# Reading the down weights of a routed expert layer in 16 KB runs, with every eighth gate and up column as stationary

## The reference, cut to what matters

```python
hid = silu(einsum('becd,edf->becf', xs, w_gate)) * einsum('becd,edf->becf', xs, w_up)
ye = einsum('becf,efd->becd', hid, w_down) * gsel[..., None]
# added back at the tokens' rows, then the gated residual; the same for both layers
```

## Time and profile before

| | |
|---|---|
| median of three runs | 1824.03 us (1822.21 to 1824.89) |
| the profiled execution's own time | 1824.63 us |
| its span, first to last instruction | 1822.8 us |
| mean granted TensorE clock | 0.972 |
| TensorE matmul busy | 1624.9 us, 89% |
| TensorE weight load busy | 1289.1 us, 71% |
| VectorE, ScalarE, GpSimd busy | 829.4, 572.0, 388.4 us |
| moved by DMA | 502.58 MB, 276 GB/s over the span |

### The profile page before, as it was taken

The page is one execution under the profiler, slowest core; times in us unless marked ns, Lnnn a source line. Parts: engine busy times, 40 slices in busy tenths (PEclk is TensorE's granted clock), DMA queues, the critical chain, the costliest instruction groups (busy, mean ns, idle before and its releaser), DMA issues. The chain is left out here.

```text
span 1822.8 us, 69666 instructions
## 1 busy us (share of the span) xinstructions
PE 1624.9 (89%) x27885; PEld 1289.1 (71%) x27885; DVE 829.4 (45%) x2593; ACT 572.0 (31%) x2234; POOL 388.4 (21%) x2149
## 2 busy tenths in 40 slices
PE   6999988986999999888869999889599998998895
PEld 3554456456999989888735454655389998998885
DVE  2299767243323333232244996852623332323233
ACT  2200245324455432221131003552354544221211
POOL 1200000001333324242210000000123342433332
PEclk9999999997999999999979999999799999999998
DMA  9356640236999999999980512220589999999993
GB/s 348 127 184 231 231 173 1 104 107 263 405 409 409 409 409 409 409 409 402 365 315 7 178 58 90 119 93 24 201 332 410 409 409 409 409 409 409 409 408 127
DMA packets 146721, 502.58 MB, mean 276 GB/s; under 512 B 6217, under 2 KB 6642, under 8 KB 146578
## 3 DMA queue, kind: packets, MB, share of 16 engines
q1 hardware_dynamic: 142288, 488.96, 68.9%
q0 software_dynamic: 3264, 10.88, 1.8%
q10 hardware_dynamic: 1026, 1.25, 0.2%
HBM read 494.76 MB, written 6.31 MB: 275 GB/s over the span
## 5 line engine op out<-in xcount | busy, mean ns | idle before, releaser
L912 PE MATMUL ps<-v_sb,weight_ring 128*64 128x80 f32 x16384 | 589.0, 234 | 55.9 <-DMA weight_ring<-in_w_gate_dram 20.2
L912 PEld LDWEIGHTS ps<-v_sb,weight_ring 128*64 128x64 f32 x16384 | 576.8, 138 | 66.9 <-DMA weight_ring<-in_w_gate_dram 24.3
L929 PE MATMUL ps<-v_sb,weight_ring 128*64 128x80 f32 x8192 | 295.2, 233 | 33.7 <-DVE v_sb L1631 20.0
L929 PEld LDWEIGHTS ps<-v_sb,weight_ring 128*64 128x64 f32 x8192 | 286.8, 137 | 42.1 <-DVE v_sb L1631 25.1
L687 PE MATMUL ps<-mix,weight_ring 128*128 128x128 f32 (+1 forms) x976 | 270.0, 438 | 2.1 <-ACT mix L1016 1.2
L1185 ACT ACTIVATE v_sb<-mix 128x8 f32 x1536 | 187.2, 205 | 227.0 <-PE ps L912 146.4
L1657 DVE TENSOR_TENSOR qk<-qk,v_sb 128x8 f32 x1520 | 212.6, 195 | 90.5 <-issue 89.7
L1780 POOL COPY v_sb<-mix 128x8 f32 x1024 | 142.9, 197 | 487.5 <-PE ps L912 430.2
L1793 POOL TENSOR_TENSOR qk<-qk,v_sb 128x8 f32 x1040 | 198.4, 232 | 182.6 <-DVE v_sb L1646 179.3
L687 PEld LDWEIGHTS ps<-mix,weight_ring 128*128 128x128 f32 x976 | 147.9, 193 | 121.9 <-issue 119.0
L1390 DVE SCALAR_TENSOR_TENSOR weight_ring<-u_gate,conv_cols,weight_ring 128x655 f32<-128x655 f32 x240 | 195.3, 896 | 0.0
(11 more groups left out here) (191 smaller groups left out, 1216.5 us busy)
## 6 DMA issues: line engine op xcount, KB each, us to landing
weight_ring<-in_w_down_dram SPq DMA_DIRECT2D x64, 2048.0 KB, 23.9
weight_ring<-in_w_gate_dram SPq DMA_DIRECT2D x48, 2048.0 KB, 20.9
weight_ring<-in_w_up_dram SPq DMA_DIRECT2D x48, 2048.0 KB, 23.8
weight_ring<-in_w_mod_dram SPq DMA_DIRECT2D x24, 2048.0 KB, 9.3
weight_ring<-in_w_in_dram SPq DMA_DIRECT2D x10, 2048.0 KB, 8.4
spare<-in_w_gate_dram SPq DMA_DIRECT2D x32, 512.0 KB, 10.5
weight_ring<-in_w_out_dram SPq DMA_DIRECT2D x4, 2048.0 KB, 9.3
rope_sb<-in_w_gate_dram SPq DMA_DIRECT2D x16, 512.0 KB, 11.3
```

Source lines behind the costliest of these rows:

```text
L912: last = nc.tensor.matmul(ps[c * HALF:(c + 1) * HALF, 2 * (i % 2) + f // BLK, f % BLK * CAP:(f % BLK + 1) * CAP], w[:, kk, o:o + HALF], pi ...
L929: last = nc.tensor.matmul(ps[c * HALF:(c + 1) * HALF, 4 + d // BLK, d % BLK * CAP:(d % BLK + 1) * CAP], w[:, kk, o:o + HALF], hid[:, k, :] ...
```

## The change

The down units are cut as `(p k)`: row `p * 8 + k` goes to partition `p`. A unit's four values of `k` are then four rows that follow one another in HBM, 16 KB for each partition, and the partitions' runs lie 32 KB apart. So that the gated hidden values lie in the same order, block `f` of the gate and up products now takes columns `f`, `f + 8`, `f + 16` and so on, 128 of them: the 64 columns of a stationary operand lie 32 bytes apart in the slot. Counts, shapes, waits, slots, the order of the queue, the down products and the sources of the gate and up units are the same.

```diff
             def expert_src(l, e, i):
                 w, half = (w_gate, w_up)[i % 2] if i < 4 else w_down, i // 2 if i < 4 else i - 4
-                return w[l, e].rearrange("(k p) n -> p k n", p=P)[:, half * 4:half * 4 + 4, :]
+                rows = w[l, e].rearrange("(k p) n -> p k n" if i < 4 else "(p k) n -> p k n", p=P)
+                return rows[:, half * 4:half * 4 + 4, :]
...
                         w = ring[:, UNIT_SLOTS[l][i], :].rearrange("p (k n) -> p k n", k=KD // 2)
+                        hidden = w.rearrange("p k (q f) -> p k f q", f=KD)
                         for f in range(KD):
                             for kk in range(KD // 2):
                                 k = (i // 2) * (KD // 2) + kk
                                 for c in range(2):
-                                    o = f * P + c * HALF
                                     last = nc.tensor.matmul(
                                         ps[c * HALF:(c + 1) * HALF, 2 * (i % 2) + f // BLK,
                                            f % BLK * CAP:(f % BLK + 1) * CAP],
-                                        w[:, kk, o:o + HALF], picked_t[:, k, :],
+                                        hidden[:, kk, f, c * HALF:(c + 1) * HALF], picked_t[:, k, :],
```

## The result

The changed kernel takes 2174.47 us (median of 4 runs, 2172.02 to 2178.7) against 1824.46 us before: ratio 1.1913, 95% interval 1.1884 to 1.1942. It is 350 us slower. The forecast was 1811, with a range from 1805 to 1843, and the case that came, the strided weight load as the bound, had 0.20.

What follows compares the result with a forecast made beforehand. The prediction took DMA's weight stream in the experts to bound the kernel. Longer down runs gave −13.3 us, all other terms nothing, so 1824.6 us became 1811.3, stated as 1811, range 1805 to 1843.

Steps and rivals of the forecast that it cites:

- the strided weight load as the bound: Gate and up products: strided columns cost twice, TensorE sets the pace instead of DMA, 2088 us; chance 0.20.
- What bounds the kernel: Experts' stream: DMA is full at 30.8 us an expert; TensorE needs 27.5, with 3.2 us to spare.
- The runs of 16 KB: Down units: one packet a run saves 0.22 us a unit, −13.3 us over 60 units.
- The addresses 32 KB apart: Down unit loads: spacing taken at nothing; as a rival, 387 GB/s, +17.4 us, 1842 us, chance 0.07.
- The lower figure: Down units: about 3 cycles (3.5 ns) overhead a packet would give −5 us; not used in the sum.
- The stationary columns 32 bytes apart: Gate and up weight loads: the stride was taken to cost nothing, though no weight load in the trace reads so.
- TensorE's clock sets their pace, not the memory: Router's weight loads: starts every 111 ns, but 211 ns at a clock of 0.50; a sign against a stride price.
- the cover of the DMA stream: Experts: 2.8 us an expert, 11 ns more a pair, would hide a column up to 45% slower.
- The hint that was set aside: VectorE's reduction: 32 values 128 bytes apart took 206 ns against 187; as a column price about 1946 us.
- The Trainium skill's rule on lines: SBUF reads: 16-byte lines need two hits for full bandwidth, new lines bring a penalty; no size given.
- the 0.80 of the other cases: Whole kernel: gain of some 13 us 0.61, no gain 0.12, slower by the new addresses 0.07.
- The rival's price: Gate and up products: 111 instead of 69.8 ns a pair, 10.6 us more an expert, 2088 us; chance 0.20.

## Why the prediction was wrong

- **What bounds the kernel.** Right, and the runs confirm it: DMA's stream bounds the kernel before, with about 3 us an expert to spare on TensorE. Half a strided unit mostly disappeared in it, two strided units did not.
- **The runs of 16 KB.** Right: 12 to 14 us at the same granted clock against 13.3, from a fixed 9.2 ns a packet (8.9 us between the medians). The lower figure worked out from the Trainium skill ("DMA: Bandwidth & Descriptors", section "Why small descriptors are slow"), −5 us, falls. The addresses 32 KB apart cost nothing that shows, at 415 GB/s.
- **The stationary columns 32 bytes apart.** This step failed: "I take nothing, as the load's own rows are nearer to this than another engine's." Behind it stood "TensorE's clock sets their pace, not the memory". That sentence is true of adjoining columns, but it says only that the memory is not slower than 0.87 ns a column when four columns share a line; it does not say how much faster it is, nor what a line costs. What the runs showed in its place: 1.8 to 1.9 ns a column when each stands on a line of its own, where a pair of 69.8 ns could bear 1.1 and the cover of the DMA stream 1.3 (80.8 / 64). The term that was put at nothing is 52 ns a pair, 13.35 us an expert.
- **The hint that was set aside.** VectorE's 0.6 ns a value more pointed the right way; it was only too small. The Trainium skill's rule on lines ("SBUF — State Buffer", section "Door 1: The DMA port swizzle") was given its rival and left at 0.20. Two sources spoke for a price, and what stood against them, the pace that follows the clock, had been read from adjoining columns alone, four to a line; no row of a strided load stood behind the 0.80 of the other cases.
- **The rival's price.** The mechanism was right, the term mis-sized: 111 ns a pair were worked out by doubling 56, and 122 measured. 256 × 11 ns × 32 experts are 90 us, which with 2088 makes 2178, against 2174.
- **What ends last.** The forecast had the unit's landing as the next thing late. That holds in the kernel with the runs alone, where TensorE waits for weight DMA; in the kernel after, TensorE's own products end last.

## What to carry to other kernels

Before a layout is changed to lengthen DMA's runs, look at who reads the data at the other end: here a step of two float32 values was free beside 80 moving columns, and from four on each weight column cost 1.8 to 1.9 ns. Compare that with the time of the moving columns, and keep the step at two or the moving operand longer than the load. With 8 KB runs and every second column the kernel keeps part of the gain, 0.9959 of the time before. Whether the gate and up units could get longer runs too, by reordering the model dimension of the gathered tokens, was not tried.

## What the runs showed of the hardware that was not expected

A strided weight load does not follow TensorE's clock. In both kernels the first products of layer 1's expert 0 run at a granted clock of 0.50; weight loads of lines 912 (before) and 913 (after) in a window of 3 us:

```profile
1321.00:1324.00 3.00, 3.00 (x48) 0.50 0.61 218
```

```profile
1492.00:1495.00 3.00, 3.00 (x48) 0.50 0.56 207
```

Both have the same 48 records; between their starts it is 133 ns a pair before and 131 after. If the strided load slowed with the clock, as the router's adjoining load does (111 to 211 ns), a pair would take some 240 ns. It takes the 133 ns of the kernel before and no more, so the load is hidden behind the moving columns; at full clock they take 67 ns and it is not. Whether it still takes 120 ns at half clock the records do not tell. So one clock state of this very kernel shows the price, and the other hides it. A check of the load's pace at half clock alone would have found the stride free.
